# Delta rule's inverse: the second form of each level's correction replaced by transposes of the placed tiles

## The reference

```python
A = jnp.where(tril & (eye == 0), jnp.einsum('bhncd,bhnsd->bhncs', kb, k) * decay, 0.0)
Tm = lax.linalg.triangular_solve(eye + A, jnp.broadcast_to(eye, A.shape), left_side=True, lower=True)
u = Tm @ (v * beta[..., None])
w = Tm @ (kb * jnp.exp(G)[..., None])
...
def step(S, xs_n):
    v_new = u_n - w_n @ S
    o = qg_n @ S + qk_n @ v_new
    S = S * gl_n[..., None, None] + jnp.swapaxes(kd_n, -1, -2) @ v_new
```

## Time and profile before

| what | value |
|---|---|
| runs, device us | 3315.38, 3301.79, 3307.10 (median 3307.1) |
| span of the profiled execution | 3315.7 us |
| PE busy, weight load busy | 3062.8 us (92%), 2911.4 us (88%) |
| DVE, ACT, POOL busy | 2161.3 us (65%), 1199.0 us (36%), 522.0 us (16%) |
| the DeltaNet stage in the span | about 1285 to 1591 us |
| its periods 2 to 5, and 6 | 28.1 us each, and 27.0 us |
| the first matmul of the next stage | 1594.4 us |

### The profile page before, as it was taken

How to read it: one execution, slowest core, us unless ns; L and a number is a source line. 1 busy time by engine, 2 the same in 40 slices (tenths; PEclk the granted TensorE clock), 3 DMA queues, 4 the chain that set the end, 5 groups by cost and what they waited for, 6 DMA issues and landing times.

```text
span 3315.7 us, 57097 instructions
## 1 busy us (share of the span) xinstructions
PE 3062.8 (92%) x23903; PEld 2911.4 (88%) x23903; DVE 2161.3 (65%) x3361; ACT 1199.0 (36%) x2108; POOL 522.0 (16%) x294
## 2 busy tenths in 40 slices
PE   7999999997988877999898899999999999999995
PEld 7999988996867655788897899999999999999995
DVE  3111777815645444366556888888888889888887
ACT  2000333104634332244223444444444444444342
POOL 2333332433460020011232000000000000000000
PEclk6999999998999987899998999999999999999997
DMA  6744245418812166022633434444444447344332
GB/s 195 224 123 126 70 131 156 139 52 279 282 66 110 71 249 190 17 89 83 169 87 93 140 116 123 122 122 123 125 126 126 126 126 237 120 144 162 97 111 105
DMA packets 517928, 443.70 MB, mean 134 GB/s; under 512 B 33168, under 2 KB 469552, under 8 KB 510750
## 3 DMA queue, kind: packets, MB, share of 16 engines
q1 hardware_dynamic: 453608, 306.83, 31.8%
q0 software_dynamic: 17488, 75.78, 6.1%
q10 hardware_dynamic: 46576, 57.44, 5.1%
HBM read 377.39 MB, written 70.93 MB: 135 GB/s over the span
## 4 chain that ended last, share of the span: by engine, by line
PE 43%; DVE 6%; DMA 1%; issue 1%; ACT 1%; ACTq 0%; DVEq 0%; SPq 0%
PE i L2537 37%; PE i L129 6%; DMA x_blocks<-s_blk 1%; DVE x_blocks L3041 1%; DVE f_half L3003 1%; DVE y_rows L3113 0%; DVE ln_parts L3047 0%; DVE y_rows L3118 0%; DVE resid L2902 0%; ACT x_blocks L2818 0%; DVE x_blocks L2916 0%; DMA x_rows<-s_h 0%; PE i L2546 0%; DVE m_lo L2849 0%; DVE h_rows L3036 0%
## 5 line engine op out<-in xcount | busy, mean ns | idle before, releaser
L2537 PE MATMUL i<-x_blocks,f_half 128*128 128x272 f32 x10752 | 1368.2, 289 | 36.6 <-DVE h_rows L3036 13.7
L2537 PEld LDWEIGHTS i<-x_blocks,f_half 128*128 128x128 f32 x10752 | 1359.4, 190 | 41.3 <-DVE x_blocks L3041 16.0
L2752 ACT CAST f_half<-w_ring 128x1024 fp32r<-128x1024 f32 (+2 forms) x370 | 346.2, 936 | 408.2 <-PE i L2537 355.5
L3003 DVE TENSOR_TENSOR f_half<-w_ring,f_half 128x1024 fp32r<-128x1024 f32 (+2 forms) x362 | 393.1, 1086 | 81.2 <-ACT f_half L2752 78.4
L129 PE MATMUL a<-x_hi,w_hi 128*128 128x272 f32 x1664 | 349.5, 291 | 18.3 <-POOL w_lo L545 18.3
L129 PE MATMUL a<-x_hi,w_lo 128*128 128x272 f32 x1664 | 345.9, 289 | 0.0
L129 PE MATMUL a<-x_lo,w_hi 128*128 128x272 f32 x1664 | 344.8, 289 | 0.0
L545 POOL TENSOR_TENSOR w_lo<-w_ring,w_hi 128x2048 fp32r<-128x2048 f32 x52 | 240.8, 4631 | 455.6 <-DVE w_hi L553 455.6
L129 PEld LDWEIGHTS a<-x_hi,w_hi 128*128 128x128 f32 x1664 | 263.5, 189 | 23.7 <-POOL w_lo L545 23.0
L129 PEld LDWEIGHTS a<-x_lo,w_hi 128*128 128x128 f32 x1664 | 263.2, 190 | 0.0
L553 DVE CAST w_hi<-w_ring 128x2048 fp32r<-128x2048 f32 x52 | 70.7, 1362 | 293.7 <-PE a L129 293.7
(11 more groups left out here) (498 smaller groups left out, 4585.8 us busy)
## 6 DMA issues: line engine op xcount, KB each, us to landing
w_ring<-in_ffn_w_up_dram SPq DMA_DIRECT2D x88, 1024.0 KB, 10.6
w_ring<-in_w_in_dram SPq DMA_DIRECT2D x52, 1024.0 KB, 6.9
w_ring<-in_ffn_w_down_dram SPq DMA_DIRECT2D x24, 1536.0 KB, 7.9
w_ring<-in_w_o_dram SPq DMA_DIRECT2D x16, 1024.0 KB, 6.0
x_blocks<-s_blk ACTq DMA_DIRECT2D x17, 816.0 KB, 5.8
s_blk<-x_sums ACTq DMA_DIRECT2D x22, 544.0 KB, 6.8
s_proj<-x_nat ACTq DMA_DIRECT2D x40, 272.0 KB, 2.6
kv_ring<-in_cmp_w_dram SPq DMA_DIRECT2D x16, 512.0 KB, 11.6
```

The source lines that it names most:

```text
L2537: last = nc.tensor.matmul(ps[bank][:, 0:HT2], half(e, j, wl_)[:, s], XB[:, x0 + s, xl_, BLK_OF[j]], start=start and s == 0 and i == 0, sto ...
L2752: nc.scalar.copy(half(e, j, 0), source(e, j)).then_inc(hq, 1)
L3003: nc.vector.tensor_tensor(half(e, j, 1), source(e, j), half(e, j, 0).bitcast(F32), ALU.subtract).then_inc(lv, 1)
```

## The change

The two matmuls per half that gave the correction transposed (L1675), and the masked write of it into TI (L2028), are gone. Instead, once DVE has placed the correction in TT, PE transposes the two TT tiles of the half (products_t), and DVE copies both whole into TI (place_turned). The last level is as before. In PE's list products_t(l) stands right ahead of products_y(l + 1), and products_y moves behind step_v. In DVE's list decay, keys_decayed and v_copy(3) are reordered around place_turned. The semaphores for y and d become counters shared by both halves.

PE's order after: y1, w_product, d1, out_rows, step_v(0), t1, y2, d2, step_s(0), step_v(1), t2, y3, rows, d3, step_s(1), step_v(2), t3, y4, keys, d4, step_s(2), step_v(3), t4, y5, d5, step_s(3), sample_s(0), turn, t5, y6, d6, sample_s(1).

DVE's order after: normed, place_d 1, mixed, v_copy(0), turned 1, decay, place_d 2, state_step(0), v_copy(1), turned 2, place_d 3, state_step(1), v_copy(2), turned 3, place_d 4, state_step(2), v_copy(3), turned 4, keys_decayed, place_d 5, state_step(3), first_level, sample_states(0), turned 5, place_d 6, turned, sample_states(1).

```diff
@@ products_d and the new products_t
                         for u in range(2):
                             last = nc.tensor.matmul(ps[dbank][:, u * P:(u + 1) * P], Y[:, 2 * a + u], TT[:, h % 3, 2 * a + u], start=True, stop=True)
-                        if l < NLV:
-                            for u in range(2):
-                                last = nc.tensor.matmul(ps[dbank][:, (2 + u) * P:(3 + u) * P], TT[:, h % 3, 2 * a + u], Y[:, 2 * a + u], start=True, stop=True)
-                        last.then_inc(d_ps[a], 1)
+                        last.then_inc(d_ps, 1)
+
+                def products_t(h, l):
+                    for a, (ybank, dbank) in enumerate(HALVES):
+                        pe.wait_ge(pl, 2 * (h * (NLV - 1) + l - 1) + a + 1)
+                        for u in range(2):
+                            last = nc.tensor.transpose(ps[dbank][:, (2 + u) * P:(3 + u) * P], TT[:, h % 3, 2 * a + u], ident)
+                        last.then_inc(pt_ps, 1)
@@ place_d and the new place_turned
                         last = nc.vector.copy_predicated(TT[:, h % 3, 2 * a:2 * a + 2], two, ps[dbank][:, 0:2 * P].rearrange("p (t c) -> p t c", t=2))
-                        if l < NLV:
-                            two = place_t[:, l:l + 1].broadcast_to((P, 2, P))
-                            last = nc.vector.copy_predicated(TI[:, h % 2, 2 * a:2 * a + 2], two, ps[dbank][:, 2 * P:].rearrange("p (t c) -> p t c", t=2))
-                        last.then_inc(inv[a] if l < NLV else inv_end, 1)
+                        last.then_inc(pl if l < NLV else inv_end, 1)
+
+                def place_turned(h, l):
+                    for a, (ybank, dbank) in enumerate(HALVES):
+                        dve.wait_ge(pt_ps, 2 * (h * (NLV - 1) + l - 1) + a + 1)
+                        nc.vector.tensor_copy(TI[:, h % 2, 2 * a:2 * a + 2].rearrange("p t c -> p (t c)"), ps[dbank][:, 2 * P:]).then_inc(inv[a], 1)
@@ PE's list, two of its places
-                    if lev is not None:
-                        products_y(lev, 3)
                     if old is not None:
                         step_v(old, 1)
+                    if lev is not None:
+                        products_t(lev, 2)
+                    if lev is not None:
+                        products_y(lev, 3)
                     if new is not None:
                         rows(new)
...
-                    if lev is not None:
-                        products_y(lev, 6)
                     if new is not None:
                         turn(new)
+                    if lev is not None:
+                        products_t(lev, 5)
+                    if lev is not None:
+                        products_y(lev, 6)
                     if lev is not None:
                         products_d(lev, 6)
```

More of the change, by code:

```diff
@@ L1836, in _ @@
                         out_rows(done)
+                    if old is not None:
+                        step_v(old, 0)
+                    if lev is not None:
+                        products_t(lev, 1)
+                    if i == 0:
+                        s_w()
                     if lev is not None:
                         products_y(lev, 2)
[L1839 to L1842, removed]
                     if lev is not None:
@@ L1848, in _ @@
                         s_out()
+                    if old is not None:
+                        step_v(old, 1)
+                    if lev is not None:
+                        products_t(lev, 2)
                     if lev is not None:
                         products_y(lev, 3)
-                    if old is not None:
-                        step_v(old, 1)
                     if new is not None:
@@ L1862, in _ @@
                         step_s(old, 1)
+                    if old is not None:
+                        step_v(old, 2)
+                    if lev is not None:
+                        products_t(lev, 3)
                     if lev is not None:
                         products_y(lev, 4)
-                    if old is not None:
-                        step_v(old, 2)
                     if i == -1:
@@ L1876, in _ @@
                         step_s(old, 2)
+                    if old is not None:
+                        step_v(old, 3)
+                    if lev is not None:
+                        products_t(lev, 4)
                     if lev is not None:
                         products_y(lev, 5)
-                    if old is not None:
-                        step_v(old, 3)
                     if lev is not None:
@@ L1889, in _ @@
                         s_o()
+                    if new is not None:
+                        turn(new)
+                    if lev is not None:
+                        products_t(lev, 5)
                     if lev is not None:
                         products_y(lev, 6)
-                    if new is not None:
-                        turn(new)
                     if lev is not None:
@@ L2152, in _ @@
                         place_d(lev, 1)
-                    if new is not None:
-                        decay(new)
                     if i == 0:
@@ L2162, in _ @@
                     if lev is not None:
+                        place_turned(lev, 1)
+                    if new is not None:
+                        decay(new)
+                    if lev is not None:
                         place_d(lev, 2)
@@ L2169, in _ @@
                         v_copy(old, 1)
+                    if lev is not None:
+                        place_turned(lev, 2)
                     if i == -1:
@@ L2188, in _ @@
                         state_step(old, 2)
+                    if old is not None:
+                        v_copy(old, 3)
+                    if lev is not None:
+                        place_turned(lev, 4)
                     if new is not None:
                         keys_decayed(new)
-                    if old is not None:
-                        v_copy(old, 3)
                     if i == 0:
```

13 lines of the change are left out of this document (9 added, 4 removed).

## The result

The changed kernel takes 3319.9 us in the median of 12 runs (3312.9 to 3328.3), the kernel before 3313.0 in the median of 12 (3301.8 to 3315.4): the ratio is 1.0031, with an interval of 1.0019 to 1.0044. That is +6.3 to +14.6 us of 3313, where +12.7 was forecast, and less than 0.5%, the case that had 0.51 of the chance. That the median came out at the forecast 3319.8 is luck: the kernel before, at 3307.1 in the three runs shown, stands at 3313.0 in twelve. The medians differ by 6.8 us and the means by 9.4, both under the 12.7.

What follows compares the result with a forecast made beforehand. PE, working in order, was taken to bound the kernel. Periods 2 to 5 +6.4, period 6 +2.6, period 7 +3.2, period 1 +1.4, period 0 -0.9 sum to +12.7 us; on the median 3307.1, 3319.8 us, range 3307 to 3335.

Steps and rivals of the forecast that it cites:

- the case that had 0.51 of the chance: Whole kernel: a change within about 0.5% (16.5 us), which a measurement cannot tell from no change; chance 0.51.
- The three kinds of wait: PE, per full period: transpose to y 3.2 us, state to step_v 1.75, y to d 0.87.
- its open question: At first_level, ahead of the turn: whether DVE or POOL's scaling goes next when POOL's copy ends; -1.0 or +0.9 us.
- The rival of POOL going first: At first_level: POOL's scaling still goes ahead, 1.9 us more per turn in periods 1 to 5, 3329.3 us; chance 0.22.
- -2.25 for work: PE, per period: 20 matmuls lost (4.45 us) and 20 transposes gained (2.2 us), -2.25 us.
- -1.0 for the second masked writes: Levels 2 to 5 of a period: y's second half no longer waits for its masked write, 4 x 0.24, -1.0 us.
- -1.0 for the turn: PE's turn, per period: its wait for first_level falls from 1.1 to 0.1 us, as DVE comes ahead of POOL's scaling.
- Periods 6 and 7: Period 6, whose turn did not wait before: +2.6 us; period 7, without `new`: +3.2 us.
- Period 8: Last period, without levels: no change counted.
- Period 1: Idle 4 us behind level 2 for the sample group, so only levels 3 to 6 count: +1.4 us.
- Period 0: First period, without `old`, partly at half clock: -0.9 us, the middle of bounds -4.5 and +2.6.
- The clock rival: PE's clock falls around sample_s, turn and t5: some 3 us each, five times at most, up to 3344 us; chance 0.14.

## Why the prediction was right, and where it was not

**The period: right, in each term.** The three kinds of wait came as worked out. From the transposes' end to y2: 1408.98 - (1407.56 + 0.44) = 0.98, predicted 0.98; to y4 1419.07 - (1418.06 + 0.44) = 0.57, predicted 0.56. From step_s to step_v 1417.40 - 1416.36 = 1.04, less its 0.45, is 0.59, predicted 0.60. From y2 to d2 1410.16 - 1408.98 = 1.18, less 0.89, is 0.29, as predicted. The sum, +1.6 for periods 2 to 5, was +1.56.

**The turn: right, and its open question is answered.** DVE and POOL after, at the end of period 2:

```profile
1427.91 0.61 POOL L1640 COPY inv_t<-consts 128x512 f32<-128x512 f32 x1 [21.58 <-PE g L1738]
1428.48 2.37 POOL L1644 TENSOR_TENSOR kv_ring<-kv_ring,gl_s 128x1024 f32<-128x1024 f32 x1
```

```profile
1428.00 0.34 DVE L2091 SCALAR_TENSOR_TENSOR state<-state,gl_p,g 128x128 f32<-128x128 f32 x1
1428.26 0.85 DVE L2071 COPY_PREDICATED inv_t<-kv_ring 128x512 f32<-128x512 int32 x1
```

first_level comes 0.35 into POOL's copy, is through in 0.85, and now the scaling is the one that is long, 2.37 where it was 1.91. So an instruction of DVE that arrives inside POOL's copy goes ahead of POOL's next: first_level takes 0.73 to 0.86 us in periods 1 to 5 of every kernel that has one write ahead of it, and 2.39 or 2.40 where there are two and the scaling stands in its place. The rival of POOL going first, 0.22 of the chance, did not happen; what it would have cost is measured by the pair of the new order with POOL's scaling in its place and later, 1.67 us a period, near the 1.9 predicted.

The Trainium skill, "SBUF — State Buffer", "SBUF: two separate sides", says that the one that starts first gets the shared pair for the whole instruction and the other blocks. The 0.85 and 2.37 after, and the 2.39 and 1.91 before, agree with it to within 0.2 us; for the case with a third instruction queued behind the first, which it does not speak of, the trace gives the answer.

**The gain, counted right but not the transposes' own.** The sum takes -2.25 for work, -1.0 for the second masked writes and -1.0 for the turn. All three came. But the hand-offs from the transposes cost 3.0 of the first two's 3.2 us again even in the old order, by the starts of its loads, and the third is POOL's and DVE's order, to be had without a transpose: the exchange alone is worth 0.24 us a period.

**Periods 6 and 7: right.** +2.5 and +3.1, predicted +2.6 and +3.2.

**Period 8: left at nothing, and two-valued.** Its work did not change, and its lengths did not in two executions; in the other two a stretch of half clock of 6.8 us added 2.8 and 2.7 us.

**Period 1: mis-sized.** The term was +1.4. The four executions took 36.9 to 37.6 us, against 36.8 to 37.3 of the kernel before and the one with decay moved: +0.3 between the means. The starts of the loads show where it lies. From step_s(1) to the end +1.3 was counted, and +1.5 came in all four (17.52 against 16.03). From the sample group's output (the first load behind the long idle stretch) to step_s(1) +0.1 was counted, but this part took 7.13 to 7.84 us, against 8.36, 7.14 and 8.31 in the three executions in the old order. Ahead of the output it is -0.25, where nothing was counted. The mis-sized part is thus y3 to d3 behind the idle stretch, which the step took at full clock; much of it stands at half clock, for 6.8 us, or 3.4 in the 7.14, and where that stretch begins and ends moves from kernel to kernel and from execution to execution.

**Period 0: mis-sized, and two-valued.** The term was -0.9, the middle of bounds of -4.5 and +2.6. It is -2.7 or +0.2. The prediction took half clock as given in that period; whether a second stretch of it comes is what makes the difference, and that changes between executions of one kernel.

**The clock rival: rightly small, but its condition was misplaced.** It did not come in periods 2 to 7 of the kernel after, in four executions. It does come in the new order alone, where the turn waits some 2 us, in three periods of five, and once in the kernel before, behind a wait of 1.1 us, so the earlier trace rows, one period of one execution, could not rule it out. Its price, set at 3 us, was 1.3, 1.4, 1.6 and 4.7.

The Trainium skill, "TensorE: Matmul & The Clock Gate", "PE-mode transpose", says that a transpose does not count as PE activity the way a matmul does. In the kernel after, t5 and the turn stand as eight transposes in a row behind matmuls of 32 rows, and the clock is 1.00 throughout the period; where it fell most, in the new order alone, the turn's four transposes stand behind a wait of 2 us. The same kernel with POOL's scaling later has the same transposes, a wait of 0.3 us and no fall, so the fall goes with the wait. Whether a transpose counts for less than a matmul no run here shows.

**The time as a whole.** The sum of +12.7 lies near the mean of the stage's difference, 12.2, and at none of its two values, 9 and 15.3. That it fits so well is in part luck: the terms of periods 0, 1 and 8 were each off by 1 to 2.8 us in one execution or another, in both directions, while periods 2 to 7 came to +11.8 (4 x 1.56 + 2.5 + 3.1) where 12.2 was forecast. The ratio's interval, +6.3 to +14.6, holds the sum. The start of the stage lies between 1294 and 1311 us in the executions of this study, with nothing changed ahead of it, so one profiled execution against one other can't confirm a sum of this size; period lengths can. The range, 3307 to 3335, was wider than the mechanism needed: its upper end, 3335, stood for POOL going first, which did not come; the clock rival at its full 3344 was not even inside it.

## What to carry to other kernels

A change that saves work on the bounding engine has to be costed together with the order it is put in: here the edit of the work gained 1.3 to 1.9 us a period and the order lost 2.9 to 3.5. The gain has to be taken apart as well: 1.0 to 1.7 of it came from DVE reaching one instruction ahead of POOL, which a move in POOL's list gives too. Where an in-order engine hands something to another and needs it back (0.31 us there, the other engine's work, 0.05 back), put a piece of work that depends on neither between the two; moving the transposes ahead of step_v, with DVE's copies moved to match, was worth 3.6 us a period, more than the edit of the work. Two hand-offs that need cover can cover each other: t, then step_v, then y.

## What the runs showed of the hardware

- An instruction of DVE that arrived 0.35 us into one POOL instruction went ahead of the next in POOL's list: 0.85 us for first_level, where behind the scaling it was 2.39 and with no scaling near 0.72. The scaling then took 2.37 instead of 1.91.
- PE's clock fell to 1.2 GHz behind an idle wait of 2 us that followed matmuls of 32 rows, in three of the five periods that had it, twice for 3.5 us and once for some 10; behind a wait of 1.1 us it fell once in fifteen. At such an edge the same list of work takes 31.5, 32.9 or 33.4 us.
- The same kernel has two lengths of period 0, 63.8 and 66.7 us, by whether a stretch of half clock falls in it, and two lengths of period 8, 20.8 and 23.5 to 23.6.
